# The MoE router of tiles 0 to 3 with its weights stationary, four contraction chunks on column groups of TensorE

## What is computed

```python
x = x + gate1 * einsum('bse,ed->bsd', o, w_out)          # output projection
h = rms_norm(x, norm2_g) * (1 + scale2) + shift2
g_logits = h @ w_grp + b_grp        # 4 groups
e_logits = h @ w_rtr + b_rtr        # 16 experts
```

## Time and profile before

| | |
|---|---|
| three runs | 1439.44, 1440.59, 1442.46 us, median 1440.59 |
| span of the profiled execution | 1439.5 us |
| its own time | not given apart; the span lies 1.1 us under the median |
| PE busy | 1272.5 us, 88% of the span |
| DVE / ACT / POOL busy | 50% / 29% / 15% |
| granted clock, mean | 0.945 of full speed |
| router matmuls L2062 | 160 instructions, both layers, five tiles |

### The profile page before, as it was taken

How to read it: one execution, slowest core, us unless ns; L and a number is a source line. 1 busy time by engine, 2 the same in 40 slices (tenths; PEclk the granted TensorE clock), 3 DMA queues, 4 the chain that set the end, 5 groups by cost and what they waited for, 6 DMA issues and landing times. The chain is left out here.

```text
span 1439.5 us, 22597 instructions
## 1 busy us (share of the span) xinstructions
PE 1272.5 (88%) x8192; PEld 758.1 (53%) x8192; DVE 717.1 (50%) x1727; ACT 411.0 (29%) x923; POOL 212.9 (15%) x305
## 2 busy tenths in 40 slices
PE   4999989999999959998959999899999994999981
PEld 3455556777767734433435554577776673444330
DVE  0344525776744535543514554367786346355442
ACT  2111135666620111111111111556665010111111
POOL 1210013010021111221111010210101111122212
PEclk9899989999999969999969999999999997999995
DMA  9700239110041797999960004580101324899955
GB/s 348 284 14 1 97 122 334 37 31 16 2 147 59 264 382 235 355 372 351 313 184 14 0 1 175 211 202 1 31 16 64 134 80 164 310 375 376 338 197 177
DMA packets 73708, 245.19 MB, mean 170 GB/s; under 512 B 6072, under 2 KB 14753, under 8 KB 60977
## 3 DMA queue, kind: packets, MB, share of 16 engines
q1 hardware_dynamic: 56080, 183.26, 34.3%
q0 software_dynamic: 17056, 58.61, 13.9%
q10 hardware_dynamic: 432, 1.36, 0.2%
HBM read 213.87 MB, written 31.00 MB: 170 GB/s over the span
## 5 line engine op out<-in xcount | busy, mean ns | idle before, releaser
L1846 PE MATMUL ps<-ring,hT_region 128*128 128x512 f32 (+1 forms) x640 | 271.7, 581 | 3.4 <-ACT hT_region L954 3.4
L1846 PEld LDWEIGHTS ps<-ring,hT_region 128*128 128x128 f32 x640 | 121.3, 193 | 135.4 <-issue 134.8
L1316 DVE TENSOR_SCALAR_CACHE_REDUCE ring<-ps 128x768 f32<-128x768 f32 (+1 forms) x168 | 132.7, 820 | 119.9 <-PE ps L1918 92.8
L1007 ACT ACTIVATE ring<-ring,negm 128x768 f32<-128x768 f32 (+1 forms) x168 | 137.7, 820 | 31.2 <-DVE ring L1316 31.2
L2042 PE MATMUL ps<-ring,hT_region 128*128 128x384 f32 (+1 forms) x480 | 141.9, 452 | 0.0
L2184 PE MATMUL ps<-ring,hT_region 128*128 x272 | 127.4, 623 | 10.3 <-SPq L587 4.4
L1918 PE MATMUL ps<-arena,qT 64*128 64x384 f32 (+1 forms) x640 | 125.7, 507 | 8.5 <-DVE ring L1316 2.9
L2042 PEld LDWEIGHTS ps<-ring,hT_region 128*128 128x128 f32 x480 | 89.6, 190 | 42.0 <-issue 0.3
L1971 PE MATMUL ps<-work,arena 128*64 128x128 f32 x1600 | 105.5, 278 | 5.9 <-ACT work L1023 4.3
L1023 ACT ACTIVATE work<-ps 128x512 f32<-128x512 f32 x128 | 75.8, 592 | 99.2 <-PE ps L1743 99.2
L1971 PEld LDWEIGHTS ps<-work,arena 128*64 128x64 f32 x1600 | 86.1, 137 | 25.2 <-issue 15.1
(11 more groups left out here) (297 smaller groups left out, 1759.6 us busy)
## 6 DMA issues: line engine op xcount, KB each, us to landing
ring<-in_w_mod SPq DMA_DIRECT2D x24, 2048.0 KB, 11.4
ring<-in_moe_w_gate SPq DMA_DIRECT2D x32, 1024.0 KB, 11.7
ring<-in_moe_w_up SPq DMA_DIRECT2D x32, 1024.0 KB, 15.3
arena<-in_moe_w_down SPq DMA_DIRECT2D x32, 1024.0 KB, 14.4
ring<-in_w_in SPq DMA_DIRECT2D x6, 2048.0 KB, 20.6
arena<-mod_rows POOLq DMA_DIRECT2D x12, 512.0 KB, 5.8
x_rows<-x POOLq DMA_DIRECT2D x10, 512.0 KB, 3.0
h_rows<-work POOLq DMA_DIRECT2D x10, 512.0 KB, 2.9
```

The costliest lines, as they stand in the source:

```text
L1007: act.activation(v, v, ACT.Exp, bias=negm[:, 2 * (k % 3) + m:2 * (k % 3) + m + 1], scale=-1.0, accum_out=sums[:, c:c + 1]).then_inc(exp_do ...
L1316: ts(o_, i_, -pair_of(p)[4], None, ALU.mult, ALU.min, accum_out=col).then_inc(m_ready, 1)
L1846: last = mm(ps[:, b, 0:n], hT[:, c, t * P:(t + 1) * P], w[:, c, :], start=(c == 0), stop=(c == KC - 1))
```

## The change

For tiles 0 to 3 the router's operands change places. `router_parts` makes 32 columns of the weights stationary (20 that count and 12 that follow them in memory) and moves the 128 tokens of `x2T` past them. Chunks `c` and `c + 4` go to column group `c % 4`, which writes PSUM partitions 32g to 32g + 31, so the four groups hold four partial sums, logits on partitions, tokens along the columns. ACT copies the 128x128 block to SBUF (`part_copy`, new). `router_sum` makes that copy stationary and moves `fold` (128x20) past it: `fold` has a one where the partition is n modulo 32, so one matmul adds the four groups and turns the result back to tokens on partitions, at `ps[:, 6, 128:148]`. DVE builds `fold` once, from the identity. `router_sum` and DVE's `logits_in` stand one block later than `router` and `logits_in` did. Tile 4 keeps the old form (`router_last`). The copies of `x2T` now wait for `rp_done` (the parts) where they waited for `rt_done`. Apart from this, three setup semaphores become one, `s_once`, with higher counts in its waits.

```diff
+        rt_part = work[:, 2432:2560]
+        rt_sum = ps[:, 6, 128:148]
+        w_rt32 = [[k_tok[:, at + 20 * c:at + 20 * c + 32] for c in range(KC)] for at in (384, 896)]
...
                 if l == 0:
-                    pool.wait_ge(s_modbias, 64)
+                    pool.wait_ge(s_once, 128)
...
+                def part_copy(t):
+                    act.wait_ge(rp_done, l * (NT - 1) + t + 1)
+                    if t >= 1:
+                        act.wait_ge(rt_done, l * NT + t)
+                    act.activation(rt_part, ps[:, 6, 0:P], ACT.Copy).then_inc(rp_evac, 1)

                 for t in range(NT - 1):
                     norm2_sums(t)
                     x2T_copy(t)
+                    part_copy(t)
...
+                    if l == 0:
+                        red(fold[:], ident[:].rearrange("p (g n) -> p n g", g=4)[:, 0:20, :], AX.X, ALU.add)
...
-                    if t >= 1:
-                        logits_in(t - 1)
                     if t == NT - 1:
                         last_copy(0)
                         scale_last(0, WO_COLS[2][0])
+                        logits_in(t - 1)
                     x_add(t, 2)
+                    if 1 <= t < NT - 1:
+                        logits_in(t - 1)
...
-                def router(t, c0, c1):
+                def router_parts(t):
+                    for c in range(KC):
+                        g = c % 4
+                        last = mm(ps[32 * g:32 * g + 32, 6, 0:P], w_rt32[min(t, 1)][c], x2T[:, c, :],
+                                  start=(c < 4), stop=(c >= 4))
+                    last.then_inc(rp_done, 1)
+
+                def router_sum(t):
+                    pe.wait_ge(rp_evac, l * (NT - 1) + t + 1)
+                    mm(rt_sum, rt_part, fold[:], start=True, stop=True).then_inc(rt_done, 1)
...
-                        router(t - 1, 0, KC)
+                        router_parts(t - 1)
                     if t == NT - 1:
                         last_T(0)
+                        router_sum(t - 1)
                     out_block(t, 2)
+                    if 1 <= t < NT - 1:
+                        router_sum(t - 1)
```

More of the change, by code:

```diff
@@ L199, in trunk @@
         sel64 = sb("sel64", 2)
+        fold = sb("fold", 20)
         cond = sb("cond", KC * 2)
@@ L334, in trunk @@
         s_cond = sem("s_cond")
-        s_modbias = sem("s_modbias")
         s_rowout = [sem(f"s_rowout{s}") for s in range(2)]
@@ L361, in trunk @@
         x_final = sem("x_final")
-        s_fill = sem("s_fill")
-        s_final = sem("s_final")
+        s_once = sem("s_once")
         s_yleft = sem("s_yleft")
@@ L415, in trunk @@
         rt_done = sem("rt_done")
+        rp_done = sem("rp_done")
+        rp_evac = sem("rp_evac")
         lg_ready = sem("lg_ready")
@@ L738, in _ @@
             for rows_ in (h_rows, *x_rows):
-                dma(rows_[0:P, :], a["x_prompt"][0]).then_inc(s_fill, 16)
+                dma(rows_[0:P, :], a["x_prompt"][0]).then_inc(s_once, 16)
             dma(lane_w[0:N_ET, :], row_b(a["step_tables"].rearrange("k m e -> (k m e)"), N_TAB * 2 * NE, N_ET)
-                ).then_inc(s_fill, 16)
+                ).then_inc(s_once, 16)
             small_load(pool, 0, 2)
@@ L745, in _ @@
                 for k in range(2):
-                    dma(mod_rows[l, k], a["b_mod"][l]).then_inc(s_modbias, 16)
+                    dma(mod_rows[l, k], a["b_mod"][l]).then_inc(s_once, 16)
             for l in range(DEPTH):
                 if l == 0:
-                    pool.wait_ge(s_modbias, 64)
+                    pool.wait_ge(s_once, 128)
                 for t in range(NT):
@@ L830, in _ @@
                 if l == 0:
-                    pool.wait_ge(s_fill, 64)
+                    pool.wait_ge(s_once, 128)
                 def y_store(i):
@@ L867, in _ @@
                     if i == 3 and l + 1 == DEPTH:
-                        dma(gain_f, row_b(a["final_norm_g"], D)).then_inc(s_final, 16)
+                        dma(gain_f, row_b(a["final_norm_g"], D)).then_inc(s_once, 16)
                 for i in range(N_ET - 3, N_ET):
@@ L883, in _ @@
                 rsqrt(rsf[:, t:t + 1], ssf[:, t:t + 1], 1).then_inc(f_rs, 1)
-            pool.wait_ge(s_final, 16)
+            pool.wait_ge(s_once, 144)
             pool.wait_ge(s_ctxout, DEPTH * 96)
@@ L1065, in x2T_copy @@
                     if t >= 1:
-                        act.wait_ge(rt_done, l * NT + t)
+                        act.wait_ge(rp_done, l * (NT - 1) + t)
                     act.activation(x2T[:, 4:8, :], ps[:, 7, :].rearrange("p (c n) -> p c n", c=4),
                                    ACT.Copy).then_inc(x2T_evac_a, 1)
+                def part_copy(t):
[3 more added lines that the diff above has]
+                    act.activation(rt_part, ps[:, 6, 0:P], ACT.Copy).then_inc(rp_evac, 1)
                 for t in range(NT - 1):
@@ L1151, in final_scale @@
             def final_scale(t):
-                dve.wait_ge(s_final, 16)
+                dve.wait_ge(s_once, 144)
                 dve.wait_ge(f_rs, t + 1)
@@ L1444, in x_add @@
                         dve.wait_ge(s_gate1, (l + 1) * 32)
-                        dve.wait_ge(s_fill, 64)
+                        dve.wait_ge(s_once, 128)
                     dve.wait_ge(wo_done, l * 15 + n + 1)
@@ L1474, in x2T_copy @@
                     if t >= 1:
-                        dve.wait_ge(rt_done, l * NT + t)
+                        dve.wait_ge(rp_done, l * (NT - 1) + t)
                     cp(x2T[:, 0:4, :], ps[:, 6, :].rearrange("p (c n) -> p c n", c=4)).then_inc(x2T_evac_d, 1)
@@ L1480, in last_copy @@
                     dve.wait_ge(lastT_done, 3 * l + n + 1)
-                    dve.wait_ge(rt_done, l * NT + NT - 1)
+                    dve.wait_ge(rp_done, (l + 1) * (NT - 1))
                     cp(x2T[:, c0:c1, :], ps[:, at, 0:(c1 - c0) * P].rearrange("p (c n) -> p c n", n=P)
@@ L1487, in logits_in @@
                     dve.wait_ge(rs2_ready, l * NT + t + 1)
-                    stt(logits[:, t, :], ps[:, 6, 0:20], rs2[:, t:t + 1], b_rt2[:, min(t, 1), :], ALU.mult, ALU.add
+                    stt(logits[:, t, :], rt_sum if t + 1 < NT else ps[:, 6, 0:20], rs2[:, t:t + 1], b_rt2[:, min(t, 1), :], ALU.mult, ALU.add
                         ).then_inc(lg_ready, 1)
@@ L2058, in x2T_rounds, with router_last @@
                         last.then_inc(x2T_done, 1)
-                def router(t, c0, c1):
+                def router_parts(t):
[7 more added lines that the diff above has]
+                    mm(rt_sum, rt_part, fold[:], start=True, stop=True).then_inc(rt_done, 1)
+                def router_last(c0, c1):
                     for c in range(c0, c1):
-                        last = mm(ps[:, 6, 0:20], x2T[:, c, :], w_rt2[min(t, 1)][:, c, :],
+                        last = mm(ps[:, 6, 0:20], x2T[:, c, :], w_rt2[1][:, c, :],
                                   start=(c == 0), stop=(c == KC - 1))
@@ L2093, in _ @@
                 pe.wait_ge(last_evac_d, 2 * l + 1)
-                router(NT - 1, 0, 3)
+                router_last(0, 3)
                 last_T(2)
                 pe.wait_ge(last_evac_a, l + 1)
-                router(NT - 1, 3, 6)
+                router_last(3, 6)
                 pe.wait_ge(last_evac_d, 2 * l + 2)
-                router(NT - 1, 6, KC)
+                router_last(6, KC)
                 pe.wait_ge(xo_done, l * 15 + 15)
```

## The result

The changed kernel took 1433.05 us in the median of 11 runs (1429.30 to 1438.05), the kernel before 1440.59 (1437.63 to 1448.02, also 11). The ratio is 0.9945, 95% interval 0.9928 to 0.9961: 7.9 us faster, between 5.6 and 10.4. The forecast was 5.6 us, 1435.0. By the ratio the time is 1432.7, just under the range that began at 1432.8; the median itself, 1433.05, lies just inside it.

What follows compares the result with a forecast made beforehand. PE was taken to bound both projection stages. Three tiles at 0.77 us plus 0.59 for tile 3 give 2.90 a layer, 5.8 for two, less 0.2 for `fold`: 5.6, from 1440.6 to 1435.0; range 1432.8 to 1438.6.

Steps and rivals of the forecast that it cites:

- What bounds the kernel: Both projection stages: PE is busy all the time, so PE time saved ends the stage earlier, one for one.
- The parts: Router of tiles 0 to 3: 16 instructions, four groups side by side, cost 0.68 us where the old router cost 1.70.
- The rate of the modulation chunk: Nearest row, 128 moving columns on four groups, two-column loads: 0.029 us an instruction, rounds of four 0.108 apart.
- Entering the parts: Start of the parts behind a 384-column block: 0.09 us, plus 0.03 for a first load that nothing hides.
- The sum: Two instructions amid full-array blocks: 0.25 us, bounds 0.14 and 0.35; wait covered in tiles 0 to 2, else 0.4 or so.
- Tile 3: Router and three transposes, 2.07 us before, take 1.48 after, PE standing 0.12 ahead of the sum: 0.59 saved.
- Tile 0: Taken like tiles 1 and 2: 1.70 - 0.68 - 0.25 = 0.77 us saved.
- 0.2 for `fold`: One small DVE reduction in the attention of layer 0, charged 0.2 us since DVE is now and then waited for there.
- B: Parts: 32-column loads go at the pace of 64-column ones, a round takes 0.22, 3.5 us more, 1438.5; 6%.
- C: Behind layer 0's stage: its gain is lost in the full DMA queue, only 2.9 less 0.2 stays, 1437.9; 9%.
- D: Stage ends earlier, but the expert half or a clock rising at another moment gives it back, 1440.6; 8%.
- E: Parts: groups don't run side by side, 2.63 us against 1.70, 0.93 lost per tile, 1448; 7%.

Runs made afterwards that it cites:

- no_cover: The changed kernel with `router_sum` directly behind `router_parts` in all four tiles; ratio to the kernel before 0.9988 (0.9963 to 1.0014).
- pair_order: The changed kernel with neighbouring chunks on the same column group (0 and 1 on group 0, and so on); ratio to the kernel before 0.9964 (0.9939 to 0.9988).
- early_sums: The changed kernel with ACT's first sum of squares of tile 4 ahead of its copy; ratio to the kernel before 0.9969 (0.9947 to 0.9991).
- early_again: The changed kernel with ACT's first tile 4 sum of squares ahead of its copy, timed again; ratio to the kernel before 0.9952 (0.9935 to 0.9969).
- one_group: The changed kernel with all eight chunks on column group 0, copy and sum over 32 partitions; ratio to the kernel before 1.0030 (1.0004 to 1.0056).

## Why the prediction was right or wrong

**What bounds the kernel: right.** PE was the bound of both stages, and saving its time shortened them, by 6.4 us together. The runs of the changed kernel are 7.9 and 6.2 us faster, so it arrived at the end.

**The parts: right.** 0.68 was forecast from block to block. The block's last matmul leaves at 451.26 (446.10 + 5.16) and the next block starts at 451.93: 0.67. The rate of the modulation chunk held although 16 times as many columns are loaded. Entering the parts costs 0.10: they start at 451.36. The Trainium skill says that a change of tiling mode drains the engine (TensorEngine Tiling (Array Packing), Key Properties); the trace agrees in kind, by that 0.10.

**The sum: right in place, a little dear.** 0.25 was taken; it starts 0.14 ahead of the next block, whose matmuls need 0.08 more (5.24 for 5.16): 0.22. No idle time in tiles 0 to 2, as forecast. `no_cover` put the cover at 0.47 in tiles 0 to 2 and 0.28 in tile 3; 0.4 was said.

**Tile 3: right.** 0.59 forecast; 2.07 became 1.29, of which 0.09 is given back ahead of the parts and 0.08 in the block behind: 0.61. Of the 0.12 for which PE was to stand ahead of the sum, 0.08 came.

**Tile 0: the term that was mis-sized.** "So tiles 0 to 2 save 1.70 - 0.68 - 0.25 = 0.77 us each" took tile 0 for a tile like the others, though the timeline of the kernel before showed it apart. Its router stands behind `factors_T`, in 64-column groups. The old router took longer there, from 435.74 to this start in the kernel before, 1.81 us and not 1.70:

```profile
437.55 2.62 PE L2042 MATMUL ps<-ring,hT_region 128*128 128x256 f32 x11
```

The parts need 0.58 there. From the first instruction of `factors_T` to the next line it is 1.90 us in either kernel (433.84 to 435.74 before, 433.81 to 435.71 after), so the parts have no 0.10 of their own to pay, as they have behind a full-array block:

```profile
435.71 0.64 PE L2077 MATMUL ps<-work,pack 128*32 128x128 f32 x16
436.29 3.72 PE L2056 MATMUL ps<-ring,hT_region 128*128 128x256 f32 x16
```

Tile 0 saved 1.00 where 0.77 was forecast. With 0.79, 0.80 and 0.61 that is 3.20 against the forecast 2.90, twice. So 6.4, not 5.8 less 0.2 for `fold`, of whose 0.2 nothing shows. Of these 0.8 tile 0 is 0.46 and `fold` 0.2.

**The range: its lower end was too near.** It allowed 2.2 us below the forecast for both the terms and the spread between runs. 0.8 went into the terms, and the 7.9 of the first comparison is 1.5 above what the stages hold. The rest of the miss is that 1.5. That it is spread, and no third effect, is supported and not proven. Five comparisons of kernels with four groups gave 7.9, 6.2, 5.2 (`pair_order`), 4.5 (`early_sums`) and 6.9 us (`early_again`), where their stages hold 6.4, 6.4, 6.1, 7.3 and 7.3: once 1.5 more, then 0.2, 0.9, 2.8 and 0.4 less. Each interval is 2.4 to 3.5 us either way, so an effect of under about 2 us outside the stages stays open.

**The rivals.** B, loads that bind: no, the parts took 0.57. The prediction laid the four loads of a round end to end, 4 x 27 ns, "just" filling it; in the trace the loads of the four groups start 0.007 us apart and last 0.11 each, so they run side by side and not one after the other. C, layer 0's gain lost: not in the queue, 3.2 went through it. D, no difference: no. E, groups that don't run side by side: no, but `one_group` shows what it would have been, 4.3 us slower by the runs and 6.0 by the stages (forecast for that case: 4.2). All 16 loads of the parts are on the same rows, and cost next to nothing beside the moving: rounds start 0.11 to 0.13 us apart, where 128 moving columns take 0.108. The rule of the Trainium skill in TensorE: Matmul & The Clock Gate (packing small matmuls), that a load overlaps matmuls only of another row group, doesn't hold here.

## What to carry to other kernels

A matmul with a full-width stationary operand and few moving columns isn't priced by its columns: the old router's instructions, 20 columns each, stood 0.112 us apart, the transposes with 128 moving columns 0.109 (eight in 0.87). That the load sets this price is likely but was not shown apart. Making the narrow operand stationary paid here only because the array's other column groups took further chunks at the same time. The partial sums then need a copy and one more matmul; standing behind other PE work was worth 3.4 of the 6.4 us. Price each place of a repeated step by what stands ahead of it there, and when a trace's stages say 6.4 and the runs 7.9, cut several traces at fixed points, look at the granted clock between them, and repeat the timing before looking for a cause.

## What the runs showed of the hardware that was not expected

- 3.5 us of matmuls with 20 moving columns, PE busy throughout, were followed by seven matmuls at 0.427 us instead of 0.216: the granted clock had gone to 1.2 GHz without a gap in PE's work. This followed five of the eight doubled routers. 1.7 us of them, as in the kernel before, left it at 1.00 in both stages.
- Four instructions in a row for one column group took about as long as two in a row: 0.59 against 0.57 us for 16.
- Weight loads of 32 columns for four column groups started 0.007 us apart, each lasting 0.11 us.
- A matmul over 32 partitions between full-array ones cost 0.33 us, one over 128 partitions 0.14.
